# Who issues the copies of the old keys and values, and where the prompt's last states are stored

## The reference

```
x = x + w_out( sigmoid(ga)*(ya @ w_br_a) + sigmoid(gb)*(yb @ w_br_b) + sigmoid(gc)*(yc @ w_br_c) )
x = x + PEER(rmsnorm(x))
```

## Time and profile before

| | |
|---|---|
| median of three runs | 3657.6 us (3653.74 to 3661.33) |
| profiled execution's own time | 3654.11 us |
| its span | 3652.3 us |
| busy: PE, DVE, ACT, POOL | 3101.7, 2292.4, 1094.2, 1175.9 us |
| DMA moved | 1313.23 MB, 360 GB/s over the span |
| mean granted TensorE clock | 0.948 of full |

### The profile page before, as it was taken

One profiled execution on the slowest core, in us unless ns is written; L12 is line 12 of the kernel. 1 busy time (PEld: TensorE's weight loads), 2 busy tenths in 40 slices (PEclk: granted clock), 3 DMA queues, 4 the chain that ended last, 5 costly groups with the idle time before them and its releaser, 6 DMA issues. The chain is left out here.

```text
span 3652.3 us, 31475 instructions
## 1 busy us (share of the span) xinstructions
PE 3101.7 (85%) x9934; PEld 1789.2 (49%) x9934; DVE 2292.4 (63%) x5227; ACT 1094.2 (30%) x3297; POOL 1175.9 (32%) x1038
## 2 busy tenths in 40 slices
PE   5699689989997889989988989988998897777777
PEld 3477554445665544446655544443665553222222
DVE  0151477885565768894565779896664577764444
ACT  0120233442222333442213333343221333332222
POOL 0000143332442333443332333442332234444433
PEclk8899899999998989999998999998999899999999
DMA  5234699988999999999999999998998799999998
GB/s 162 87 95 139 253 406 379 416 350 351 415 420 353 418 377 421 420 386 373 420 419 357 407 372 414 387 388 318 417 420 311 296 355 416 421 421 421 421 422 355
DMA packets 204456, 1313.23 MB, mean 360 GB/s; under 512 B 23282, under 2 KB 27434, under 8 KB 71641
## 3 DMA queue, kind: packets, MB, share of 16 engines
q0 software_dynamic: 148608, 1082.20, 72.9%
q1 hardware_dynamic: 49111, 213.07, 15.3%
q10 hardware_dynamic: 6570, 15.94, 1.3%
HBM read 1294.81 MB, written 17.61 MB: 359 GB/s over the span
## 5 line engine op out<-in xcount | busy, mean ns | idle before, releaser
L1974 POOL DMA_INDIRECT arena<-uv,eidx x1032 | 1175.4, 1139 | 2448.2 <-PE ps L894 1785.9
L894 PE MATMUL ps<-arena,dgs 128*128 128x512 f32 x3308 | 1575.9, 618 | 300.3 <-ACT dgs L1227 280.9
L1518 DVE CUSTOM_DVE_ANT_0 arena<-arena,xx 128x1024 f32<-128x1024 f32 x1024 | 1239.9, 1222 | 650.9 <-DMA arena<-uv,eidx 622.3
L894 PEld LDWEIGHTS ps<-arena,dgs 128*128 128x128 f32 x3308 | 626.4, 196 | 1065.5 <-issue 629.6
L1208 ACT ACTIVATE gel<-dots 128x2 f32<-128x2 f32 x516 | 104.4, 202 | 1448.3 <-DVE dots L1518 1447.5
L930 PE MATMUL ps<-wbuf,xT 128*128 128x420 f32 (+1 forms) x1152 | 428.5, 521 | 56.9 <-ACT arena L1284 41.2
L930 PEld LDWEIGHTS ps<-wbuf,xT 128*128 128x128 f32 (+1 forms) x1152 | 204.9, 180 | 280.6 <-issue 261.3
L1105 PE MATMUL ps<-xT,wbuf 128*128 128x256 f32 (+1 forms) x1344 | 318.3, 391 | 12.4 <-DMA wbuf<-w_merge 10.9
L1227 ACT ACTIVATE dgs<-cst,wgt 128x128 f32<-128x128 f32 x827 | 297.7, 396 | 16.7
L1105 PEld LDWEIGHTS ps<-xT,wbuf 128*128 128x128 f32 x1344 | 261.2, 196 | 80.1 <-DMA wbuf<-w_merge 22.2
L1478 DVE SCALAR_TENSOR_TENSOR xx<-arena,wgt,xx 128x1024 f32<-128x1024 f32 x197 | 252.3, 1281 | 66.7 <-ACT wgt L1220 66.6
(11 more groups left out here) (361 smaller groups left out, 1965.3 us busy)
## 6 DMA issues: line engine op xcount, KB each, us to landing
wbuf<-w_merge SPq DMA_DIRECT2D x84, 768.0 KB
wbuf<-w_z SPq DMA_DIRECT2D x64, 840.0 KB
wbuf<-w_q SPq DMA_DIRECT2D x64, 512.0 KB
arena<-uv,eidx POOLq DMA_INDIRECT x1032
wbuf<-w_o SPq DMA_DIRECT2D x32, 512.0 KB
xin<-x_prompt SPq DMA_DIRECT2D x8, 1024.0 KB, 11.1
wbuf<-w_merge SPq DMA_DIRECT2D x12, 512.0 KB
grow<-gains SPq DMA_DIRECT2D x8, 512.0 KB, 8.8
```

Of the source, the lines that this page charges most:

```text
L894: done = mm(ps[:, half, :], dgs[:, j, :], ring[:, j, row_], start=(q == 0), stop=(q == P - 1), skip_group_check=True)
L1518: v.tensor_tensor_reduce(ring[:, j, 0:D], ring[:, j, 0:D], x, 1.0, 0.0, ALU.mult, ALU.add, dots[:, j:j + 1]).then_inc(s["dotted"], 1)
L1974: g.indirect_dma_start(ring[:, j, :], None, uv, bass.IndirectOffsetOnAxis(ap=experts, axis=0)).then_inc(got[j], 16)
```

## The change

`load_caches` moves from ScalarE, behind unit 3 of the first projection, to GpSimd, ahead of its first gather: GpSimd runs it as soon as two memsets and their wait are done. Its five DMAs are the same in shape; all of them now count on one new semaphore, `caches_in`. The waits that counted them elsewhere are split accordingly. `store_last_state` leaves the list of the last w_o loads and is called once all weight loads have been issued, ahead of SP's wait for the samples' output.

```
@@ sample_tensor
             point(LAST, "x", 0)
-            pe.wait_ge(s["k_load"], 16 * 4)
+            pe.wait_ge(s["caches_in"], 16 * 5)
+            pe.wait_ge(s["k_load"], 16 * 2)
@@ block.sync
-                weights(w_o, (HALF, OC), NO, s["o_mm"], NO * tiles_before(p), tiles, [store_last_state] if p == LAST else [])
+                weights(w_o, (HALF, OC), NO, s["o_mm"], NO * tiles_before(p), tiles)
...
                 weights(w_q, (KC, P), 2 * PH, s["kq_mm"], 2 * PH * p, 1, [lambda: load_x(p + 1)] if p < LAST else [])
+            store_last_state()
             sp.wait_ge(s["sample_y"], 1)
             sp.dma_start(y_s, xin_s).then_inc(s["y_out"], 16)
-            sp.wait_ge(s["outs"], 16 * 4)
+            sp.wait_ge(s["outs"], 16 * 3)
+            sp.wait_ge(s["caches_in"], 16 * 5)
             sp.wait_ge(s["state_stored"], 16)
             sp.wait_ge(s["state_c_stored"], 16 * 4)
-            sp.wait_ge(s["kscr"], 16 * 4)
+            sp.wait_ge(s["kscr"], 16 * 2)
@@ block.scalar, project
-                    if p == 0 and c == 3:
-                        load_caches()
@@ block.gpsimd
             g.memset(vprev[:, :], 0.0).then_inc(s["init_p"], 1)
             pool.wait_ge(s["init_p"], 1)
+            def load_caches():
+                for rows_, cache, out in ((Ks, cache_k, k_s), (Vs, cache_v, v_s)):
+                    pool.dma_start(rows_[0:W - 1, :, :], cache[:, 1:W, :].rearrange("n k c -> k n c")).then_inc(s["caches_in"], 16)
+                    pool.dma_start(out[:, 0:W - 1, :], cache[:, 1:W, :]).then_inc(s["caches_in"], 16)
+                pool.dma_start(pool_s[:, 0:HIST - 1, :], state_pool[:, 1:HIST, :]).then_inc(s["caches_in"], 16)
+            load_caches()
```

More of the change, by code:

```diff
@@ L147 @@
 state_out_tr state_out_sb consts_in early_out
-outs w_in0 w_in1 kept zs_out zs_in xs_in sample_y state_stored state_c_stored b_n c_load sel_in bsel_in smp_out c_round0 c_round1 c_round2 c_round3 k_load kscr smp_a smp_p smp_v
+outs w_in0 w_in1 kept zs_out zs_in xs_in sample_y state_stored state_c_stored b_n c_load sel_in bsel_in smp_out c_round0 c_round1 c_round2 c_round3 k_load caches_in kscr smp_a smp_p smp_v
 stats_v topk_v""".split()
@@ L1249, in norm @@
                       ps[:, b:b + 2, :].rearrange("p a (c n) -> p a c n", c=4)[:, :, :, 0:rows_], ACT.Copy).then_inc(s["xT_ready"], 1)
[L1251 to L1256, removed]
             def spread_bias():
```

## The result

The changed kernel takes 3624.2 us, median of four runs (3621.7 to 3629.9), against 3659.5 (3653.7 to 3662.6) of the kernel before on the same chip: 35.3 us less. The ratio on record is 0.9907 with a 95% interval of 0.9894 to 0.9919 (the two medians alone give 0.9904). The forecast was 3602, its range 3585 to 3617. The direction was right, the time lies 7 us above the range.

The account below looks back on a forecast made before the run. A first pass of some 425 us without gathers, engines following one another, then a long part moving expert rows, its tail DMA-full. 3654.1 - 45 (parts 1 and 2) - 8 (part 3) = 3601.1, 3604.6 from the median; forecast 3602, range 3585 to 3617.

Parts of the forecast that it names:

- Part 1: First projection: cache loads leaving ScalarE remove TensorE's wait for evacuation and some w_z waiting, 46.9 us (43.3 to 60.4).
- rival E: First projection: the caches, not biasfull's spread, held unit 4, so the remaining 13.5 us go too, 3588 us; chance 0.16.
- Part 2: Start of the first pass: the same five cache transfers on GpSimd make tables or weights late, costing 2 us (0 to 16).
- the spread case: Start of the first pass: cache transfers spread over engines, end by 20 us, cost one or two us.
- Rival C: First projection: caches keep one engine on GpSimd too, 7 us of waits come, net about 37, 3610 us; chance 0.17.
- Part 3: Last pass: moving state stores from between w_o loads gains 12 us, costs 4 in the DMA-full tail, net 8.
- rival A: ScalarE's cache issuing: only issue time is saved, some 2 us plus 8, 3644 us; chance 0.04.

Follow-up runs that it names:

- e3: The changed kernel with each cache load into SBUF cut into 112 and 15 partitions, still on GpSimd: 3605.6 us, 0.9852 of the kernel before.
- e4: The changed kernel, loads uncut, with GpSimd's cache DMAs held back until the first projection has been evacuated: 3625.8 us, 0.9902 of the kernel before.
- e6: e3 with biasfull's spread issued behind unit 3 in place of unit 1: 3605.9 us in one run.
- e1: The kernel before with only the cache loads moved to GpSimd, state stores left between the w_o loads: 3632.9 us against 3658.2, 0.9943.
- e5: The kernel before with only each cache load into SBUF cut into 112 and 15 partitions, ScalarE still issuing: 3606.5 us against 3657.8, 0.9859.
- e8: e3 with n_p alone stored again between the second and third w_o load of the last pass: 3626.4 us, timed once.
- e9: e3 with c_p and m_p stored again between the w_o loads, n_p behind the last weight load: 3604.6 us, timed once.

## Why the prediction was wrong

**The bound and the lever: right, as far as the scatter shows.** What went before the first gather came through: 22.4 us at the first gather and 11.9 net at the stores are 34.3, the timed gain 35.3.

**Part 1: right.** With the cache loads out of the way (e3, e4) the projection ends at 121 to 122 us, "near 120" as forecast: e4's 121.3 is 46.0 us under the 167.3 of before, where the sum had 46.9. The spread, not the caches, holds unit 4: e4 and e6 show it, and rival E is out. It keeps all of its 12.3 us there, where I took 1.3 off. In the changed kernel itself the sign I had named, 9 to 13 us at unit 4, did not come: 5.18, with waits at seven other places.

**Part 2: this is the step that failed**, where it says "I take 2, nearest the spread case". No row bore out that case. The term measures 24.7 us: the projection ends at 146.0 with the five transfers in it and at 121.3 without (e4); by e1's 141.3 it is 20.0. With them TensorE has seven waits of 2.2 to 5.2 us and one of 1.1, and over 9 us of slow units behind them, in place of the spread's one wait. The loads did not spread: their rows went one at a time, 39 us for the keys and 41 for the values. Net of parts 1 and 2, 22 came in place of 45, and the first gather at 402.4 in place of 378, beyond the 390 that I had called wrong. Rival C had the shape (waits at many units); its 37 net was 15 too high, and even the upper bound, 16, lies 9 under the 24.7. Two errors are in that bound. It took unit 6's 2.31 us, one wait, for the most a unit can pay, and the waits here go to 5.18; and it left out what I had counted for the other waits in the same text, that TensorE comes back slow. Beside it, the reading of the 79.9 us stopped at "one engine, so the issuer is held": that names the load's shape as the cause, and the change keeps the shape. e5 shows what follows: cutting 127 rows into 112 and 15 takes most of the hold away where it is.

The Trainium skill, "DMA: Bandwidth & Descriptors", the section on the increment by 16, has the rule for SP and ScalarE as the rows have it: one engine for 127 partitions. Its exception for GpSimd, some direct copies on all 16 engines with 8 partitions each, is not what ran here: the 254 packets of 4096 bytes went one at a time, as one engine would take them.

**Part 3: right in kind, 2 to 4 us too low.** The gain at w_o was 12.9 (forecast 12), the price in the tail 1 to 3 us (forecast 4), so 10 to 12 net in place of 8. Pass 1's unit costs 4.10 + 6.35 - 3.62 = 6.8, not 6.7, which changes nothing. n_p's words are the main cause (e8); I had not seen that c_p and m_p hold a load too (e9).

**The rule against the change**, in the Trainium skill, "DMA: Bandwidth & Descriptors", section "Issuing engines are not separate DMA queues", is that issuing elsewhere saves only the sequencer's time, usually small. Here that time was not small: ScalarE was held 79.9 us, and rival A is out. The same section says that the transfers of all issuers run on the same 16 engines, and that took about half of the gain, 20.0 to 24.7 of 46.0 us.

## What to carry to other kernels

When an engine is held at issuing a DMA, look at the shape of the transfer ahead of it in the queue, before looking for another issuer: here 127 rows cut into 112 and 15 gained 51 us with nothing moved (e5), the move alone 25 (e1). A transfer moved to an idle queue keeps its hold on the DMA engines; price it by every load that passes it, each wait with the slow restart of TensorE behind it. Stores of single words belong where no load that someone is waiting for comes next in the same queue.

## What the runs showed of the hardware

- A load of 127 x 8 x 512 bytes held ScalarE's queue 50.74 us (behind the spread) and 28.10 us, GpSimd's 42.24; as 112 + 15 rows, the two pieces of one went out in 1.7 us on GpSimd, with no hold behind them, and both loads in 16.3 us with their copies on ScalarE, behind the spread.
- Whole, in GpSimd's queue, its rows of 4096 bytes went one at a time (two overlapped for 1.3 of 55 us), with 15 packets of 32 bytes for each row that the cut load does not have: 0.18 of the DMA share at 21 GB/s.
- 1 MB read from 8 partitions took 22 us on the way to DRAM and stopped a weight load for 12 us; as eight DMAs it filled the engines (0.83 of the share for 89 GB/s) and took 37 us.
- 512 stores of one word, 2 KB, made the load behind them in SP's queue 12.3 us late in place of the usual 2.0, and 256 KB of c_p with m_p 7.58; all of them beside gathers cost 1 to 3 us.
